# Transformer layer on one core: output projection as three fp32r products of split parts, second norm folded into the router, residual rows turned directly

## The reference

```python
mix = jnp.concatenate([ret, att], axis=-1) * mix_scale
x = x + g1[:, None, :] * (mix @ w_o)
h2 = rms_norm(x, norm2_g) * (1.0 + sc2[:, None, :]) + sh2[:, None, :]
y = moe(h2.reshape(B * S, D), router_w, router_b, w_gu, b_gu, w_down, b_down).reshape(B, S, D)
# in moe:
logits = (h @ router_w + router_b).astype(jnp.float32)
top_vals, top_idx = lax.top_k(logits, TOP_K)
```

## Time and profile before

| | |
|---|---|
| median of 3 runs | 1601.48 us |
| lowest and highest | 1601.24, 1601.77 us |
| profiled execution, its own time | 1605.01 us |
| profiled execution, its span | 1603.2 us |
| mean granted clock of TensorE | 0.959 of full speed |

### The profile page before, as it was taken

One profiled execution on the slowest core, in us unless ns is written; L12 is line 12 of the kernel. 1 busy time (PEld: TensorE's weight loads), 2 busy tenths in 40 slices (PEclk: granted clock), 3 DMA queues, 4 the chain that ended last, 5 costly groups with the idle time before them and its releaser, 6 DMA issues.

```text
span 1603.2 us, 20619 instructions
## 1 busy us (share of the span) xinstructions
PE 1489.5 (93%) x6872; PEld 1185.7 (74%) x6872; DVE 1329.3 (83%) x1153; ACT 1085.5 (68%) x1126; POOL 422.0 (26%) x341
## 2 busy tenths in 40 slices
PE   3999996896799999999999999999999999999993
PEld 3667963455588888888888888888888888888872
DVE  4689957366599999998999999998999999998992
ACT  3554325333677777788877777788877777788881
POOL 1113510101113322233223322233223423233221
PEclk8899987996899999999999999999999999999996
DMA  9745510225499999999999999999999999999974
GB/s 348 219 156 184 184 54 14 60 79 202 177 365 372 364 364 373 374 370 382 360 372 371 370 365 372 370 375 379 357 378 370 376 348 370 382 379 368 362 272 132
DMA packets 95983, 483.70 MB, mean 302 GB/s; under 512 B 23416, under 2 KB 32752, under 8 KB 43632
## 3 DMA queue, kind: packets, MB, share of 16 engines
q1 hardware_dynamic: 83200, 450.47, 72.2%
q0 software_dynamic: 12752, 32.84, 8.6%
HBM read 469.09 MB, written 23.61 MB: 307 GB/s over the span
## 4 chain that ended last, share of the span: by engine, by line
PE 83%; DVE 9%; ACT 3%; DMA 3%; issue 1%; SPq 0%; POOLq 0%; DVEq 0%; POOL 0%; ACTq 0%
PE bank L1364 15%; PE bank L1363 15%; PE bank L1365 15%; PE bank L1385 7%; PE bank L1387 7%; PE bank L1386 7%; PE bank L1246 3%; PE bank L1344 2%; PE bank L1356 2%; PE bank L1336 2%; DVE w_lo L1474 2%; DMA ring<-in_ada_w 1%; PE bank L1067 1%; PE bank L1068 1%; PE bank L1069 1%
## 5 line engine op out<-in xcount | busy, mean ns | idle before, releaser
L1513 DVE TENSOR_TENSOR e_lo<-ring,e_hi 128x2048 fp32r<-128x2048 f32 x384 | 868.4, 2289 | 93.9 <-ACT e_hi L742 93.4
L742 ACT ACTIVATE e_hi<-ring 128x2048 fp32r<-128x2048 f32 x384 | 728.5, 1914 | 235.8 <-PE bank L1365 234.6
L1363 PE MATMUL bank<-e_hi,x_hi 128*128 128x512 f32 x1024 | 405.9, 396 | 1.6 <-DVE e_lo L1513 1.6
L1364 PE MATMUL bank<-e_lo,x_hi 128*128 128x512 f32 x1024 | 402.5, 393 | 0.0
L1365 PE MATMUL bank<-e_hi,x_lo 128*128 128x512 f32 x1024 | 398.8, 389 | 0.0
L1363 PEld LDWEIGHTS bank<-e_hi,x_hi 128*128 128x128 f32 x1024 | 192.7, 188 | 48.4 <-DVE e_lo L1513 2.5
L1364 PEld LDWEIGHTS bank<-e_lo,x_hi 128*128 128x128 f32 x1024 | 193.1, 189 | 40.0
L1365 PEld LDWEIGHTS bank<-e_hi,x_lo 128*128 128x128 f32 x1024 | 192.8, 188 | 40.2
L1385 PE MATMUL bank<-e_hi,act_hi 128*128 128x512 f32 x512 | 208.5, 407 | 0.1
L1387 PE MATMUL bank<-e_hi,act_lo 128*128 128x512 f32 x512 | 201.9, 394 | 0.0
L1386 PE MATMUL bank<-e_lo,act_hi 128*128 128x512 f32 x512 | 201.1, 393 | 0.0
(11 more groups left out here) (247 smaller groups left out, 1800.4 us busy)
## 6 DMA issues: line engine op xcount, KB each, us to landing
ring<-in_w_gu SPq DMA_DIRECT2D x256, 1024.0 KB, 8.6
ring<-in_w_down SPq DMA_DIRECT2D x128, 1024.0 KB, 7.3
ring<-in_ada_w SPq DMA_DIRECT2D x24, 1024.0 KB, 7.3
ring<-in_w_in SPq DMA_DIRECT2D x9, 1024.0 KB, 5.9
ring<-in_w_o SPq DMA_DIRECT2D x4, 1024.0 KB, 7.6
ring<-in_w_in SPq DMA_DIRECT2D x10, 256.0 KB, 5.9
sum_rows<-xs POOLq DMA_DIRECT2D x5, 512.0 KB, 4.5
xs<-in_x SPq DMA_DIRECT2D x4, 512.0 KB, 4.9
```

What stands on the lines that cost most here:

```text
L742: return nc.scalar.activation(dst, src, ACT.Copy, scale=scale)
L1363: pe.matmul(bank[b][:], x_hi[:, c, :], hi, start=False, stop=False)
L1364: pe.matmul(bank[b][:], x_hi[:, c, :], lo, start=False, stop=False)
L1513: tt(e_lo[c % PARTS][:], raw(period.raw_slot(c)), e_hi[:, c % PARTS, :].bitcast(F32), ALU.subtract).then_inc(lo_ready, 1)
```

## The change

- The mix is written as two fp32r tensors, `mix_hi` (ACT) and `mix_lo` (DVE, eight `mix_rest`). `w_o` is split likewise, `wo_hi` by four ACT copies of 128x2048 (into ring slots 4 and 5 and two parts of `e_hi`) and `wo_lo` by four DVE subtractions in place.
- `mixed` makes three fp32r products for each k, in the order 0, 1, 2, 3, 4, 6, 5, 7.
- The scale of the second norm goes into `rw`, its shift into `rb` through a new PE step `router_bias`; the factor of each row is applied in `choose`.
- PE turns `xs` itself; ACT copies the result with two operations of 128x512 (`turned_rows_out`) in place of eight of 128x128. `normal` is parted into `root` and `normal`.
- The router's loads wait for the last `mix_rest`; the first expert's pieces 0 and 1 wait for `wo_used`.

```diff
-AFTER_MIX = [f"o{t}{q}" for t in range(T - 1) for q in range(2)] + ["l0", "o30", "c0", "l1", "o31"]
+AFTER_MIX = ["o00", "rb"] + [f"o{t}{q}" for t in range(T - 1) for q in range(2)][1:] + ["l0", "o30", "c0", "l1", "o31"]
+MIX_ORDER = [0, 1, 2, 3, 4, 6, 5, 7]
...
-                    elif c == 0:
-                        sp.wait_ge(g_stored, 16)
-                    elif 2 <= c < 5:
-                        sp.wait_ge(wo_used, c - 1)
+                    elif c < 5:
+                        sp.wait_ge(wo_used, (1, 2, 1, 2, 3)[c])
...
-            pool.wait_ge(act_taken, A_MIX + RH)
-            pool.wait_ge(values_taken, 4)
+            pool.wait_ge(mix_lo_ready, KD)
             pool.dma_start(rw, router_w.rearrange("(k p) e -> p k e", p=P)).then_inc(router_in, 16)
...
+            def wo_hi_part(n):
+
+                r = LOAD_O[n]
+                a.wait_ge(landed[r % SLOTS], 16 * (r // SLOTS + 1))
+                if n == 0:
+                    a.wait_ge(g_stored, 16)
+                if n == 2:
+                    a.wait_ge(values_full, 3)
+                copy(wo_hi[n], slot(r)).then_inc(wo_hi_ready, 1)
+
+            wo_hi_part(0)
+            wo_hi_part(1)
             for i in range(STEPS + VALUE_LAG):
...
+                if i == STEPS + 2:
+                    wo_hi_part(2)
+                    wo_hi_part(3)
                 if TURN_LAG <= i < STEPS + TURN_LAG:
                     turned(i - TURN_LAG)
...
+            root(0)
             normal(0)
+            turned_rows_out(0)
+            root(1)
             normal(1)
-            h2(0)
-            h2(1)
+            turned_rows_out(1)
...
-                free(j)
+                if k == RH - 1:
+                    pe.wait_ge(mix_hi_ready, 3)
+                    pe.wait_ge(mix_lo_ready, 3)
...
-                    mm = pe.matmul(dbank(j)[:], hT[:, k, t * P:(t + 1) * P], w[:, k % 2, q * 512:(q + 1) * 512],
-                                   start=(k == 0), stop=(k == KD - 1))
+                    mm = exact(dbank(j)[:], mix_hi[:, k, rows], mix_lo[:, k, rows], wo_hi[k // 2][:, cols],
+                               wo_lo[k // 2][:, cols], n == 0, n == KD - 1)
...
+            def router_bias():
+
+                pe.wait_ge(router_in, 32)
+                pe.wait_ge(affine_ready, 2)
+                j = D_["rb"]
+                dfree(j)
+                for k in range(KD):
+                    mm = pe.matmul(dbank(j)[:, 0:E], modB[:, k:k + 1].broadcast_to((P, P)), rw[:, k, :],
+                                   start=(k == 0), stop=(k == KD - 1))
+                mm.then_inc(dve_full, 1)
...
             mixed(0, 0)
+            router_bias()
             mixed(0, 1)
...
+            wo_lo_part(0)
+            wo_lo_part(1)
             v.wait_ge(ro_full, RH)
             for i in range(STEPS + TURN_LAG):
...
+                if i == STEPS:
+                    mix_rest(2, 0, abank(A_MIX)[:])
                 if i >= TURN_LAG:
                     turned(i - TURN_LAG)
+                if i - VALUE_LAG == 2 * T:
+                    mix_rest(0, 4, bank[6][:])
+                    mix_rest(1, 6, bank[7][:])
+            for k in range(1, RH):
+                mix_rest(2 + k, k, abank(A_MIX + k)[:])
+            wo_lo_part(2)
+            wo_lo_part(3)
+            mix_rest(6, 5, bank[6][:])
+            mix_rest(7, 7, bank[7][:])
```

More of the change, by code:

```diff
@@ L74 @@
 A_H2 = A_MIX + RH
+NOT_TAKEN = RH
 D_RG = 0
@@ L399, in landed @@
                 return raw_in[s], self.i * 32 + 16 * (c // SLOTS + (1 if s >= 4 else 0))
+        wo_hi = [ring_r[:, 4 * SLOT:5 * SLOT], ring_r[:, 5 * SLOT:6 * SLOT], e_hi[:, 0, :], e_hi[:, 1, :]]
+        wo_lo = [ring_r[:, n * SLOT:(n + 1) * SLOT] for n in range(4)]
         def rows_of(t):
@@ L896, in values_out @@
                     k = 4 + 2 * n + half
-                    copy(hT[:, k, :], bank[6 + n][:], vecT[:, 64 + k:65 + k]).then_inc(values_taken, 1)
+                    copy(mix_hi[:, k, :], bank[6 + n][:], vecT[:, 64 + k:65 + k]).then_inc(mix_hi_ready, 1)
             def retention_out(k):
@@ L918, in _, with root @@
             values_out(1)
-            def normal(t):
+            def root(t):
                 a.wait_ge(x2_ready, 2 * t + 2)
@@ L924, in normal, with turned_rows_out @@
                                      bias=epsc[:]).then_inc(rms_root, 1)
+            def normal(t):
                 a.wait_ge(rms_inv, 2 + t)
                 copy(xn2[:, t, :], xs[:, t, :], ri[:, t:t + 1]).then_inc(xn2_ready, 1)
-            def h2(t):
+            def turned_rows_out(t):
+                if t >= 2:
+                    a.wait_ge(dve_full, D_[f"l{t - 2}"] + 1)
                 for half in range(2):
@@ L931, in h2 @@
                     a.wait_ge(act_full, j + 1)
-                    for q in range(4):
-                        k = 4 * half + q
-                        last = affine(hT[:, k, t * P:(t + 1) * P], abank(j)[:, q * P:(q + 1) * P], a2[:, k:k + 1],
-                                      modB[:, k:k + 1])
-                    last.then_inc(act_taken, 1)
+                    copy(x2T[:, t % 2, 4 * half:4 * half + 4, :],
+                         abank(j)[:].rearrange("p (k n) -> p k n", k=4)).then_inc(act_taken, 1)
+            root(0)
             normal(0)
+            turned_rows_out(0)
+            root(1)
             normal(1)
-            h2(0)
-            h2(1)
+            turned_rows_out(1)
+            root(2)
             normal(2)
-            h2(2)
+            turned_rows_out(2)
+            root(3)
+            turned_rows_out(3)
             normal(3)
-            h2(3)
             def hi(period, c):
@@ L1240, in mixed @@
                 dfree(j)
-                for k in range(KD):
-                    n = LOAD_O[k // 2]
-                    if (t, q) == (0, 0) and k % 2 == 0:
-                        have(n)
-                    w = slot(n).rearrange("p (k n) -> p k n", k=2)
-                    mm = pe.matmul(dbank(j)[:], hT[:, k, t * P:(t + 1) * P], w[:, k % 2, q * 512:(q + 1) * 512],
-                                   start=(k == 0), stop=(k == KD - 1))
-                    if (t, q) == (T - 1, 1) and k % 2 == 1 and k < KD - 1:
+                for n, k in enumerate(MIX_ORDER):
+                    if (t, q) == (0, 0):
+                        pe.wait_ge(mix_lo_ready, (6, 6, 6, 6, 6, 6, 8, 8)[n])
+                        pe.wait_ge(wo_lo_ready, k // 2 + 1)
+                    rows, cols = slice(t * P, (t + 1) * P), slice((k % 2) * D + q * 512, (k % 2) * D + q * 512 + 512)
+                    mm = exact(dbank(j)[:], mix_hi[:, k, rows], mix_lo[:, k, rows], wo_hi[k // 2][:, cols],
+                               wo_lo[k // 2][:, cols], n == 0, n == KD - 1)
+                    if (t, q) == (T - 1, 1) and k in (1, 3, 5):
@@ L1252, in turn_rows @@
             def turn_rows(t):
-                pe.wait_ge(xn2_ready, t + 1)
+                pe.wait_ge(x2_ready, 2 * t + 2)
                 for half in range(2):
                     j = A_H2 + 2 * t + half
-                    free(j)
+                    if j >= A_H2 + 3:
+                        pe.wait_ge(act_taken, j - 2 - NOT_TAKEN)
                     for q in range(4):
                         at = (4 * half + q) * P
-                        mm = pe.transpose(abank(j)[:, q * P:(q + 1) * P], xn2[:, t, at:at + P], ident[:])
+                        mm = pe.transpose(abank(j)[:, q * P:(q + 1) * P], xs[:, t, at:at + P], ident[:])
@@ L1606, in turned, with wo_lo_part, mix_rest @@
                                                                           n=P)).then_inc(turned_odd, 1)
+            def wo_lo_part(n):
+                v.wait_ge(wo_hi_ready, n + 1)
+                tt(wo_lo[n], slot(LOAD_O[n]), wo_hi[n].bitcast(F32), ALU.subtract).then_inc(wo_lo_ready, 1)
+            def mix_rest(n, k, src):
+                v.wait_ge(mix_hi_ready, n + 1)
+                stt(out=mix_lo[:, k, :], in0=src, scalar=vecT[:, 64 + k:65 + k], in1=mix_hi[:, k, :].bitcast(F32),
+                    op0=ALU.mult, op1=ALU.subtract).then_inc(mix_lo_ready, 1)
+            wo_lo_part(0)
+            wo_lo_part(1)
             v.wait_ge(ro_full, RH)
@@ L1643, in choose @@
                 v.wait_ge(dve_full, j + 1)
-                tt(lgt[:, t, :], dbank(j)[:, 0:E], rb[:], ALU.add).then_inc(dve_taken, 1)
+                stt(out=lgt[:, t, :], in0=dbank(j)[:, 0:E], scalar=ri[:, t:t + 1], in1=rb[:], op0=ALU.mult,
+                    op1=ALU.add).then_inc(dve_taken, 1)
                 v.wait_ge(dve_taken, j + 1)
@@ L1693, in _ @@
             residual(0, 0)
+            j = D_["rb"]
+            v.wait_ge(dve_full, j + 1)
+            tt(rb[:], rb[:], dbank(j)[:, 0:E], ALU.add).then_inc(dve_taken, 1)
+            v.wait_ge(dve_taken, j + 1)
+            tt(rw, rw, a2[:].unsqueeze(2).broadcast_to((P, KD, E)), ALU.mult).then_inc(rw_ready, 2)
             residual(0, 1)
```

25 lines of the change are left out of this document (15 added, 10 removed).

## The result

The changed kernel took 1607.97 us (median of 6 runs, 1605.47 to 1613.3), the kernel before 1601.34 us (6 runs, 1599.46 to 1601.77). The ratio is 1.0038, with a 95% interval of 1.0023 to 1.0054: 6.6 us slower. The forecast was 1608.8, the range 1603.3 to 1613.0.

A forecast was written before the change was run, and what follows sets the result against it. PE was taken to bound the kernel (93% busy, 83% of the chain). Terms +9.25 + 0.8 - 5.8 + 2.2 + 1.9 + 1.7 + 0.2 - 1.5 - 1.45 = +7.3 on 1601.5 gave 1608.8 us, range 1603.3 to 1613.0.

The forecast's parts named there:

- The products: Output projection: each `mixed` falls from 6.93 to 5.5 us; only some of the eight count on the chain, sum -8.75 us.
- The rival in which they run at the fp32 price: Split products in `mixed` cost as much as fp32, so the 8.75 us gain is gone: +16, 1617.5 us; chance 2%.
- First half of the split: Two ACT copies and two DVE subtractions of `w_o` ahead of the attention, hidden by nothing: +5.4 us (4.5 to 5.7).
- The rests in step 13 and 16: Late attention: DVE's `mix_rest` wait for ACT's copies and delay its next step, +1.95, and retention block 3's turn, +1.0 us.
- Second half: ACT copies the other half of `w_o` between turned(14) and turned(15), so values(3) starts later: +2.3 us.
- The clock there: Half clock around values(3) after PE's idle time, 1.6 us, half taken back by the router's wait: +0.8 (0 to 1.6).
- The router: After mixed(0,0), PE waits for the router's loads, +2.2 us (bounds 1.0 and 4.5), then runs `router_bias`, +1.9 us.
- The fall of the clock in mixed(0,1): PE, having done little for over 4 us around the router's wait, runs mixed(0,1) at lower clock: +1.7 us (0 to 1.8).
- mixed(3,0) and (3,1): Last tile's projection: mixed(3,0), restarting after a DVE wait half at lower clock, gains 1.5 us; mixed(3,1) gains 1.45.
- absorption: Rival: slack between the attention's steps takes up the first half's 5.4 us, giving 1603.4 us, no change; chance 11%.
- full clock throughout: Rival: TensorE is granted full clock everywhere, bringing back 13.7 us and giving 1595.1 us; chance 4%.
- loads that take twice as long: Rival: router loads land after twice 3.4 us (+3.4) and clock falls take full price (+1.8): +12.5, 1614.0 us; chance 8%.

The follow-up runs named there:

- e_bias: Changed kernel with the seven `bias_parts` operations spread over the gaps between the residuals where DVE waits for PE: 1605.38 us, ratio 1.002 to the kernel before.
- b_bias: Kernel before the change, with only `bias_parts` spread over the gaps between the residuals: 1597.47 us, ratio 0.997 to the kernel before.
- e_again: The changed kernel once more, no edit, beside the kernel before: 1611.2 us, ratio 1.0057.
- e_front: Changed kernel with the first half of the `w_o` split moved from ahead of the attention into gaps between retention heads: 1603.52 us, ratio 1.0012.
- e_best: As e_all_late, with retention block 3 turned after values(2) on PE and one step later on ACT: 1590.54 us, ratio 0.993 to the kernel before.
- e_all_late: Changed kernel with the edits of e_front, e_router and e_bias, plus ACT's second-half `w_o` copies after the last `turned`: 1591.02 us, ratio 0.9941.
- e_router: Changed kernel with the router's loads issued once the last attention logits are taken, not after the last rest: 1609.12 us, ratio 1.0046.

## Why the prediction was right, step by step

**The products.** 5.57 to 5.64 us for a `mixed` at full clock (forecast 5.5), from 6.8 to 6.93. Three products took 0.69 us, where 0.68 had been read off those of the experts. Counted together the term was too big: the first four `mixed` gave 5.1 us (5.8 forecast; 5.7 by the prediction's own 27.72 - 22), mixed(3,1) 1.34 (1.45) and mixed(3,0) 1.51 (1.5), in all 7.95 in after where 8.75 had been summed. Timeline of PE, changed kernel, two neighbouring groups of three:

```profile
317.08 0.39 PE L1095 MATMUL bank<-ring_r,mix_hi 128*128 128x512 f32 x1
...
317.77 0.40 PE L1095 MATMUL bank<-ring_r,mix_hi 128*128 128x512 f32 x1
```

The rival in which they run at the fp32 price is out. The claim that only part of the eight counts is shown by the pair e_bias and b_bias.

**First half of the split: right.** Step 0 came 5.17 us later (forecast 5.4), values(0) started 5.02 us later in after and 5.39 in e_again, and e_front gave about 5 of it back. The duration of the copies and subtractions was read off the experts' rows and held: 3.70 for two copies, 2.28 for one subtraction. One sign of being wrong was badly put: "DVE's step 0 starts before 249" is a time from the start of the span, and so are 307 for values(3) and 310.5 for the first product. In after they were 246.62, 303.35 and 307.34, all too early by the letter, since this execution reached the last head 3.89 us earlier than before's. Only the distances from that head answer what the sign was meant to ask.

**The rests in step 13 and 16: right as a sum.** DVE waited 0.70 us for ACT's copy before the first rest:

```profile
287.06 1.41 DVE L1657 SCALAR_TENSOR_TENSOR mix_lo<-bank,vecT,mix_hi 128x512 fp32r<-128x512 f32 x2 [0.70 <-ACT mix_hi L750]
```

and block 3 waited 1.29 us in place of 0.38, 0.9 more where 1.0 was forecast; e_best shows that this wait was on the path. Both lie between the starts of values(1) and values(2): 13.31 us before, 16.15 in after and in e_again, with values(1) at 4.06 to 4.07 us in all three. That is 2.84 more; forecast were 1.95 + 1.0 = 2.95.

**Second half: +2.3 forecast, 2.06 measured** as the difference of PE's wait ahead of values(3), 2.93 against 0.87, and confirmed by e_all_late. In after:

```profile
303.35 4.06 PE L1236 MATMUL bank<-prT,area 128*64 128x512 f32 x16 [2.93 <-ACT prT L750]
```

**The clock there: mis-sized.** I had charged 0.8 of the 1.6 us, on the argument that the router's wait takes half of it back. It takes nothing back: in the chain above, ACT's last copy, the last two rests, POOL's issue and the load of `rb` all follow values(3) one behind the other, so what makes values(3) late makes the load late as well. values(3) took 4.00 to 4.07 us in five of the six traces that have the wait (3.64 in e_front), and 2.37 or 2.38 in all four that don't: before, b_bias, e_all_late, e_best. Window of after:

```profile
303.40:307.40 4.00, 4.00 (x17) 1.66 (x17) 4.00 (x2) 0.00 (x0) 0.00 (x0) 0.57 0.00 0
```

The projection's start came out nearly to the forecast all the same, +10.0 us in after (67.0 behind the head, 56.98 in before) where 9.25 + 0.8 had been worked out. That is luck in part: the stretch up to values(0) fell 0.4 short, the rests 0.1, the second half 0.2, values(0) was 0.2 us shorter than in before, and the clock at values(3) went 0.9 over. mixed(0,0) no longer waits for ACT's last copies, as foreseen.

**The router: over-sized by 0.8.** 2.2 + 1.9 = 4.1 us were forecast, and `residual(0,0)` to `residual(0,1)` less one `mixed` is 8.90 - 5.57 = 3.3. The wait was 1.33 us, `router_bias` 1.97:

```profile
314.50 1.97 PE L1287 MATMUL bank<-area,modB 128*128 128x32 f32 x16 [1.33 <-DMA rb<-in_router_b]
```

What was mis-sized is the start of POOL's issue: the last rest ended 2.3 us after the start of mixed(0,0), not 3.0, and POOL began 0.28 us behind it, not 0.6. The landing was nearly right. From the start of its issue the load took 3.66 us here, 3.76 in e_again, 3.63 in e_front and 3.84 in e_bias, where 3.4 had been read the earlier trace rows. The Trainium skill (DMA: Bandwidth & Descriptors, Anatomy of one DMA) gives such a load about 2.0 us; by the pages of all ten kernels it took 3.1 to 3.8 us, which speaks against that figure for this transfer.

**The fall of the clock in mixed(0,1)** was forecast at 1.7 (0 to 1.8). It came in e_again, 1.6, and not in after, e_front and e_bias, which have the wait too; the bounds were right, and as a single value 1.7 was too much. The spread of the kernel's runs, 1605.5 to 1613.3, is four fifths as wide as the prediction's whole range, which a single profiled run could not show.

**residual(1,1) to residual(2,0): 17.73 us in before, after and e_again.** The 0.2 for ACT's new order were nothing. That this distance is to the hundredth the same with cheap and with dear products is the clearest sign that DVE sets it.

**mixed(3,0) and (3,1).** From `residual(2,1)` to `residual(3,1)` 17.87 us before, 15.02 in after, 15.79 in e_again, where the clock was low in 354 to 361; forecast -2.95, measured -2.85 and -2.08.

**The tail.** From `residual(3,1)` to the first expert's product 37.99 us before, 38.09 in e_again, 38.0 in e_router: unchanged, as forecast. In after it was 36.78, and 0.9 of the difference is in one row, places(1) at 1.16 us (374.09 in the chain above) against 2.08, the same eight instructions at another clock. Windows over places(1), first after, then e_again:

```profile
374.00:375.30 1.30, 1.21 (x11) 1.21 (x11) 1.13 (x8) 1.30 (x2) 1.20 (x3) 1.00 1.02 429
```

```profile
378.80:381.00 2.20, 2.15 (x10) 2.15 (x11) 1.45 (x7) 2.20 (x2) 1.16 (x3) 0.50 1.03 410
```

**Sum.** Forecast +7.3; from the last head to the first expert's product +4.15 in after, +6.7 in e_again; on the medians +6.6 in the first comparison and +9.4 in the second. In after the 3.15 us that are missing to the forecast are: the start of the projection 0.1, the router 0.8, ACT's order 0.2, the fall in mixed(0,1) 1.7 and the tail 1.2, less 0.8 that the products gave too little. In e_again it is 0.6: the start of the projection came 1.2 early (values(0) at full clock), the router was 0.7, ACT's order 0.2 and the fall 0.1 too big, and the other way the products of the first four 0.7, mixed(3,0) and (3,1) 0.9 and the tail 0.1. The mechanisms held; what lies between 4.15 and 6.7 is where the clock fell in the one execution and in the other. That the first comparison came out within 0.7 us of the forecast is luck in part: the trace of its own shortest run gives 3.15 us less than the forecast, and the second comparison +9.4, which no trace accounts for in full. Of the rivals, absorption is excluded by e_front and the fp32 price by the products' rows; full clock throughout came in no trace; loads that take twice as long neither.

## What to carry to other kernels

A cheaper product of split operands brings only what is left after its preparation: put every copy and subtraction where its engine waits anyway (here beside the retention heads and behind the last step of the attention). Here a loss of 6.6 to 9.4 us became a gain of 6.9 us against b_bias. Before making one engine faster, look in the chain for the stretches that another sets; here moving `bias_parts` into DVE's waits was worth 4.4 us by itself. When a kernel's profiled run lies at an edge of its spread, compare distances from a common event, not spans, and look at the same instructions in both for the clock before you put a difference down to an edit.

## What the hardware showed that was not expected

- A wait of PE that is 2.06 us longer cost 3.75 us: the 16 instructions behind it took 4.06 us at a granted clock of 0.57 and 2.37 us at 1.00. Of the six traces with the longer wait none shows these instructions at full clock, of the four without it all do. A long wait is not needed for a low clock, though: values(1) took 4.06 to 4.07 us in nine of the ten traces and 3.81 in e_front, and values(2), 2.37 or 2.38 elsewhere, took 3.96 in e_front.
- The same program shows a fall of the clock in one execution and not in the next (values(0): 3.89 us in after, 2.37 in e_again; mixed(0,1) the other way round), and its runs spread over 7.8 us (0.5%), where the kernel before stayed within 2.3 us in the same comparison; in the second, with 20 runs, it spread over 5.4 us.
- A transfer of 16 KB issued by POOL landed 3.63 to 3.84 us after the start of its issue in the four traces in which PE waits for it, more than the 2.8 to 2.9 us of the 128 KB one issued ahead of it, as before.
